# Loading x after the last memory units, and working the first two weight units as single k-tiles, in a two-layer decoder trunk on one Trainium2 core

## The reference

```python
def reference(x, mem, ...):
    for i in range(DEPTH):                       # DEPTH = 2
        h = _rms_norm(x, pre_norm[i])
        proj = h @ w_in[i]                       # 2048 x 7168
        ...                                      # short conv (layer 0) or differential attention (layer 1)
        mem_n = _rms_norm(mem, mem_norm[i])
        kv = mem_n @ w_kv_mem[i]                 # keys: columns 0-511, values: columns 512-1023
        ...                                      # cross-attention of 4 heads
        branch = jnp.concatenate([tok_out, cross_out], axis=-1) * jax.nn.silu(gate)
        x = x + _rms_norm(branch @ w_out[i], post_norm[i])
    return x
```

## Time and profile before

| what | value |
|---|---|
| time, median of 3 runs | 963.57 us (959.42 to 963.98) |
| time of the profiled execution | 964.46 us |
| its span, first to last instruction | 962.7 us |
| PE busy | 947.7 us, 98% of the span |
| PE weight loads busy | 813.1 us |
| DVE busy | 630.4 us |
| ACT busy | 475.4 us |
| moved by DMA | 182.31 MB, 189 GB/s in the mean |
| mean granted TensorE clock | 0.997 |

### The profile page before, as it was taken

How to read it: one execution, slowest core, us unless ns; L and a number is a source line. 1 busy time by engine, 2 the same in 40 slices (tenths; PEclk the granted TensorE clock), 3 DMA queues, 4 the chain that set the end, 5 groups by cost and what they waited for, 6 DMA issues and landing times.

```text
span 962.7 us, 14077 instructions
## 1 busy us (share of the span) xinstructions
PE 947.7 (98%) x5148; PEld 813.1 (84%) x5148; DVE 630.4 (65%) x867; ACT 475.4 (49%) x725; POOL 1.2 (0%) x9
## 2 busy tenths in 40 slices
PE   8899999999999999999999999999999999999996
PEld 7788888888888888888888888888888888888885
DVE  5677666656665656645596447457778878886555
ACT  6756634344434343344465445445465465554441
POOL 0000000000000000000000000000000000000000
PEclk9999999999999999999999999999999999999998
DMA  9657555666666656655666655565655765646562
GB/s 330 203 171 260 174 176 178 191 191 192 189 191 181 189 179 191 205 192 194 199 203 201 183 169 179 171 197 167 205 167 162 219 184 164 200 148 203 192 196 89
DMA packets 148762, 182.31 MB, mean 189 GB/s; under 512 B 8112, under 2 KB 116976, under 8 KB 147952
## 3 DMA queue, kind: packets, MB, share of 16 engines
q1 hardware_dynamic: 147776, 177.25, 59.2%
q10 hardware_dynamic: 944, 4.49, 1.2%
HBM read 176.48 MB, written 2.10 MB: 185 GB/s over the span
## 4 chain that ended last, share of the span: by engine, by line
PE 95%; DMA 2%; DVE 1%; ACT 0%; SPq 0%; issue 0%; DVEq 0%; ACTq 0%
PE psum L368 40%; PE psum L369 20%; PE psum L428 10%; PE psum L430 10%; PE psum L429 10%; DMA stage_area<-in_mem_dram 1%; PE psum L604 1%; PE psum L447 1%; PE psum L472 1%; PE psum L455 1%; DMA raw_ring<-in_w_kv_mem_dram 1%; DVE lo_ring L914 1%; PE psum L576 0%; PE psum L464 0%; ACT hi_ring L653 0%; PE psum L586 0%
## 5 line engine op out<-in xcount | busy, mean ns | idle before, releaser
L368 PE MATMUL psum<-hT_split,hi_ring 128*128 128x512 f32 x1600 | 564.4, 398 | 0.0
L914 DVE TENSOR_TENSOR lo_ring<-raw_ring,hi_ring 128x1024 fp32r<-128x1024 f32 x319 | 386.1, 1223 | 256.8 <-ACT hi_ring L653 255.0
L653 ACT ACTIVATE hi_ring<-raw_ring 128x1024 fp32r<-128x1024 f32 x319 | 336.4, 1062 | 398.1 <-PE psum L369 262.0
L369 PE MATMUL psum<-hT_split,lo_ring 128*128 128x256 f32 x1600 | 447.2, 279 | 0.0
L368 PEld LDWEIGHTS psum<-hT_split,hi_ring 128*128 128x128 f32 x1600 | 300.3, 188 | 72.8 <-issue 2.0
L369 PEld LDWEIGHTS psum<-hT_split,lo_ring 128*128 128x128 f32 x1600 | 301.7, 189 | 0.1
L428 PE MATMUL psum<-hi_ring,branchT_split 128*128 128x512 f32 x256 | 99.9, 390 | 0.0
L430 PE MATMUL psum<-hi_ring,branchT_split 128*128 128x512 f32 x256 | 99.6, 389 | 0.0
L429 PE MATMUL psum<-lo_ring,branchT_split 128*128 128x512 f32 x256 | 99.6, 389 | 0.0
L430 PEld LDWEIGHTS psum<-hi_ring,branchT_split 128*128 128x128 f32 x256 | 48.1, 188 | 10.1
L429 PEld LDWEIGHTS psum<-lo_ring,branchT_split 128*128 128x128 f32 x256 | 48.1, 188 | 10.0
(11 more groups left out here) (186 smaller groups left out, 671.8 us busy)
## 6 DMA issues: line engine op xcount, KB each, us to landing
raw_ring<-in_w_in_dram SPq DMA_DIRECT2D x224, 512.0 KB, 4.5
raw_ring<-in_w_out_dram SPq DMA_DIRECT2D x64, 512.0 KB, 4.9
raw_ring<-in_w_kv_mem_dram SPq DMA_DIRECT2D x31, 512.0 KB, 4.6
layer_area<-layer_area SPq DMA_DIRECT2D x48, 64.0 KB, 3.2
stage_area<-in_mem_dram SPq DMA_DIRECT2D x8, 256.0 KB, 7.1
x_residual<-in_x_dram SPq DMA_DIRECT2D x2, 1024.0 KB, 9.7
x_residual<-in_x_dram ACTq DMA_DIRECT2D x1, 2048.0 KB, 10.1
layer_area<-in_post_norm_dram ACTq DMA_DIRECT2D x2, 1024.0 KB, 5.4
```

Of the source, the lines that this page charges most:

```text
L368: mm(o, hi[:, k, P * c:P * (c + 1)], X[:, kt, :], start=kt == 0, stop=False)
L369: last = mm(o[:, SEQ:], lo[:, k, P * c:P * (c + 1)], X[:, kt, 0:SEQ], start=False, stop=kt == KT - 1)
L653: run(whi[:, slot, :], raw[:, slot, :], ACT.Copy).then_inc(hi_ready, 1)
L914: V_.tensor_tensor(wlo[:, slot, :], raw[:, slot, :], whi[:, slot, :].bitcast(f32), SUB)\
```

## The change

Three things are altered, all in `first_keys` and in what ACT, DVE and PE do beside it.

1. `load_x(0)` moves behind unit 6, `load_x(1)` behind unit 7.
2. Unit 1 is treated as unit 0 was: two DMAs of 256 KB, two split halves on ACT and on DVE, two k-tiles on PE with the transposes for unit 2 between them (before: ahead of the unit). The low parts of its two `memT_split` tiles have separate signals.
3. At the very start ACT splits the first half of unit 0 ahead of its norm wait and of `turned(0)`, and DVE takes the low part of that half ahead of the low part of the first tile. The second half of unit 0 is then split after `turned(0)`; on DVE it comes after both tiles.

```diff
-            load_mem(0)
-            sp.dma_start(raw[:, 0, 0:CROSS_WIDTH], w[:, 0, :]).then_inc(unit_begun, 16)
-            sp.dma_start(raw[:, 0, CROSS_WIDTH:], w[:, 1, :]).then_inc(raw_loaded[0], 16)
-            for n in range(1, STEPS):
+            for n in range(2):
+                load_mem(n)
+                sp.dma_start(raw[:, n, 0:CROSS_WIDTH], w[:, 2 * n, :]).then_inc(unit_begun[n], 16)
+                sp.dma_start(raw[:, n, CROSS_WIDTH:], w[:, 2 * n + 1, :]).then_inc(raw_loaded[n], 16)
+            for n in range(2, STEPS):
                 load_mem(n)
                 unit(n, n % SLOTS, raw[:, n % SLOTS, :].rearrange("p (k c) -> p k c", k=K_KT),
                      w[:, K_KT * n:K_KT * (n + 1), :])
-                if n in (5, 6):
-                    load_x(n - 5)
+                if n in (6, 7):
+                    load_x(n - 6)
...
-            pe.wait_ge(tile_turned, 1)
-            pe.wait_ge(lo_begun, 1)
-            k_tile(0, 0, range(4))
-            mem_turn(1)
-            pe.wait_ge(tr_lo, N_MEM0 + 1)
-            pe.wait_ge(lo_ready, 1)
-            k_tile(0, 1, range(4)).then_inc(unit_done, 1)
-            for n in range(1, STEPS - 1):
+            for n in range(2):
+                pe.wait_ge(tile_turned, n + 1)
+                pe.wait_ge(lo_begun, n + 1)
+                k_tile(n, 0, range(4))
+                mem_turn(n + 1)
+                pe.wait_ge(tr_lo, N_MEM0 + n + 1)
+                pe.wait_ge(lo_ready, n + 1)
+                k_tile(n, 1, range(4)).then_inc(unit_done, 1)
+            for n in range(2, STEPS - 1):
...
+        def first_high(n, half):
+            act.wait_ge(raw_loaded[n] if half else unit_begun[n], 16)
+            part = slice(CROSS_WIDTH * half, CROSS_WIDTH * (half + 1))
+            run(whi[:, n, part], raw[:, n, part], ACT.Copy).then_inc(hi_ready if half else hi_begun, 1)
+
+        first_high(0, 0)
         act.wait_ge(norm_ready, 1)
         turned(N_MEM0, XB, 2 * KT)
-        act.wait_ge(unit_begun, 16)
-        run(whi[:, 0, 0:CROSS_WIDTH], raw[:, 0, 0:CROSS_WIDTH], ACT.Copy).then_inc(hi_begun, 1)
-        act.wait_ge(raw_loaded[0], 16)
-        run(whi[:, 0, CROSS_WIDTH:], raw[:, 0, CROSS_WIDTH:], ACT.Copy).then_inc(hi_ready, 1)
+        first_high(0, 1)
         keep(0)
-        for n in range(1, STEPS):
+        first_high(1, 0)
+        turned(N_MEM0 + 1, XB, 2 * KT)
+        first_high(1, 1)
+        for n in range(2, STEPS):
...
-        dve.wait_ge(tr_hi, 1)
-        first_tile(0).then_inc(tile_turned, 1)
-        first_low(0)
-        first_tile(1).then_inc(tr_lo, 1)
-        first_low(1)
-        for n in range(1, STEPS):
+        first_low(0, 0)
+        first_tile(0, 0)
+        first_tile(0, 1)
+        first_low(0, 1)
+        first_low(1, 0)
+        first_tile(1, 0)
+        first_low(1, 1)
+        first_tile(1, 1)
+        keep(1)
+        for n in range(2, STEPS):
```

More of the change, by code:

```diff
@@ L188, in build @@
     mem_rows_loaded, pre_rows_loaded = sem("mem_norm_loaded"), sem("pre_norm_loaded")
-    unit_begun, hi_begun, lo_begun = sem("first_unit_half"), sem("first_hi_half"), sem("first_lo_half")
-    keys_half, tile_turned = sem("first_keys_half_done"), sem("first_tile_turned")
+    unit_begun = [sem(f"unit{n}_first_half") for n in range(2)]
+    hi_begun, lo_begun = sem("first_hi_halves"), sem("first_lo_halves")
+    keys_half, tile_turned = sem("first_keys_half_done"), sem("first_tiles_turned")
     gpost_loaded, out_stored = sem("gpost_loaded"), sem("out_stored")
@@ L999, in op, with first_tile, first_low @@
             st.need()
[L1001 to L1008, removed]
+        def first_tile(n, k):
+            dve.wait_ge(tr_hi, n + 1)
+            kt = 2 * n + k
+            V_.scalar_tensor_tensor(XB[:, kt, 256:512], ps[:, 4 + n, 256 * k:256 * (k + 1)],
+                                    gT[:, 2 * KT + kt:2 * KT + kt + 1], XB[:, kt, 0:256].bitcast(f32), MULT, SUB)\
+              .then_inc(tr_lo if k else tile_turned, 1)
+        def first_low(n, half):
+            dve.wait_ge(hi_ready if half else hi_begun, n + 1)
             part = slice(CROSS_WIDTH * half, CROSS_WIDTH * (half + 1))
-            V_.tensor_tensor(wlo[:, 0, part], raw[:, 0, part], whi[:, 0, part].bitcast(f32), SUB)\
+            V_.tensor_tensor(wlo[:, n, part], raw[:, n, part], whi[:, n, part].bitcast(f32), SUB)\
               .then_inc(lo_ready if half else lo_begun, 1)
```

## The result

The changed kernel takes 956.09 us (median of 6 runs, 955.9 to 956.39) where the kernel before, run again beside it, takes 964.1 (959.42 to 965.21, 6 runs): a ratio of 0.9919, with an interval of 0.9905 to 0.9933. The forecast was 961.6 and no measurable change; the medians lie 8.0 us apart. The times of the kernel before fall into two groups, 958.0 to 960.4 and 963.1 to 965.8 (one of its 121 executions lies between them), within every series of runs, and five of the six here are of the upper group. I call them the lower and the upper group.

What follows compares the result with a forecast made beforehand. PE was taken as the bound behind the first 37.64 us; there 3.2 us for the stall minus 1.2 for the head gave 2.0 us, moving the median from 963.57 to 961.6 us, range 957.8 to 964.2.

Steps and rivals of the forecast that it cites:

- The step that failed: PE, busy behind the first 37.64 us, is the bound; only that start can change, its saving passing unaltered to the end.
- the runs scatter: Rival: one of three runs took 959.42, four microseconds under the others; a median falling there gives 957.4 us; chance 0.15.
- The start: First 37.64 us: 3.2 us gained for the stall minus 1.2 for the head, 2.0 us in all.
- the last matmuls of the start move as a whole: From ACT's third sum of squares (26.67) to the first memory values matmul (37.64), one chain shifts unchanged, to 35.6.
- x behind the units: Unit 7's features, with one megabyte of x ahead instead of two, land at 23.9; ACT's 3.19 us stall goes to nothing.
- The new start: Reordered head: PE's first matmul 0.6 us later (8.47 for 7.85), ACT 1.21 us behind from unit 2's kept copy on.
- A second transfer for unit 1: The extra SP transfer costs nothing seen; a fixed 2.0 us in line, kept as rival, would leave a gain of 0.8 us.
- Unit 8: Landing left at 30.3, needed by about 32.0; rival: it becomes late, gain gone at 34.0, 965.6 us at 36; chance 0.06.
- the clock: Rival: PE's longer pause before its first k-tile lowers its clock, ending 4.7 us later at 968.3 us; chance 0.04.

Runs made afterwards that it cites:

- e6: Changed kernel with 17 instead of 16 transposes ahead of the mixer's loop of layer 0; ten executions at 961.1 to 962.2 us.
- e13: Changed kernel with 17 transposes ahead of the loop and one fewer idle transpose at the start; ten executions at 961.0 to 964.1 us.
- e4: Kernel before with 17 instead of 16 transposes ahead of the loop of layer 0; ten executions at 963.4 to 965.7 us.
- e11: Changed kernel with 17 transposes ahead of the loop and one small product behind them; ten executions at 961.0 to 962.8 us.
- e8: Kernel before with one small product (128x256) between the 16 transposes and the loop; ten executions at 958.2 to 960.3 us, ratio 0.9972.
- e9: Changed kernel with one small product between the 16 transposes and the loop; median 957.19 us of six, ratio to the kernel before 0.9937.
- e10: Changed kernel with a small product ahead of the loop and of layer 1's first keys' and first query groups; six executions at 956.3 to 958.7 us.
- e5: Changed kernel run again unaltered, beside the kernel before on the same chip; seven executions at 955.8 to 957.2 us, one at 961.4.
- e2: Changed kernel with x's transfers back behind units 5 and 6; nine executions at 958.4 to 961.4 us, one at 963.9.
- e7: Kernel before with 18 instead of 16 transposes ahead of the loop; six executions at 958.5 to 959.8 us, four at 963.8 to 965.2.
- e16: Changed kernel with PE's old order at unit 1, transposes for unit 2 first; seven executions at 956.1 to 958.0 us, three at 961.2 to 962.8.
- e3: Changed kernel with the old order of ACT and DVE at the very start; nine executions at 956.5 to 957.2 us, one at 961.8.
- e1: Kernel before with only x's two transfers moved behind units 6 and 7; four executions at 956.1 to 957.8 us, six at 961.1 to 962.4.

## Why the prediction was wrong

**The step that failed** is the first: "So only the first 37.64 us can change, and whatever they save or lose passes unaltered to the end: PE is the bound behind them." PE is the bound behind them, but being busy is not a fixed pace. The loop has two, and the profiled execution of before ran at the long one. 5.1 us of the 8.0 come from that. In the sum this term stood nowhere. The rival "the runs scatter" touched it and gave 957.4 with a chance of 0.15; it took the 959.42 for noise, where it was the other pace. The trace of before could have said so: the group ahead of the transposes, from 101.0 us on, runs its pairs at 346.7 ns, the loop behind them at 353.3. Three pairs of that group, to be held against the first four rows of the pattern above (1.04 us here, 1.06 there):

```profile
102.42 0.39 PE L368 MATMUL psum<-hT_split,hi_ring 128*128 128x512 f32 x1
...
103.46 0.39 PE L368 MATMUL psum<-hT_split,hi_ring 128*128 128x512 f32 x1
```

**What the runs showed in its place.** The pace of the loop is taken on at the restart behind the 16 transposes and kept for all 768 pairs (e6, e13). It is drawn in each execution, and its odds belong to the code. The short pace came in 54 of 121 for the kernel before, 13 of 14 for the changed one, none of 40 with 17 transposes (e4, e6, e11, e13), 22 of 22 with 16 transposes and a product (e8, e9, e10). So the comparison of medians had luck in it, too: one kernel was measured mostly in its upper group and the other in its lower one. With the medians of its two groups and its own odds the kernel before has 0.45 x 959.2 + 0.55 x 963.9 = 961.8 in the mean, and the changed kernel's fourteen executions have 956.6. The change is worth 5.2 us in the mean: 2.9 from the start (959.2 to 956.3, lower group against lower group) and 2.3 from the draw.

**The start** was sized nearly right, at 2.0 us. Within one series, that with e5, the lower groups are 958.6 and 956.3, 2.3 us apart, and the upper groups of before and of e6 963.8 and 961.6, again 2.3; in that of the result it is 964.2 - 956.1 less the 5.1 of the pace, 3.0. The step that the last matmuls of the start move as a whole is borne out best: in all eighteen traces the memory values begin 10.96 to 11.00 us behind the start of ACT's third sum of squares. That sum begins at 25.6 to 27.5 in the seven traces with x in its old place (26.5 in the mean) and at 23.2 to 25.5 in the eleven with x behind the units (24.3 in the mean, forecast 24.7), so the 3.5 us between the two profiled executions hold, by an estimate from these means, about 1.2 us of scatter. By steps:

- *x behind the units*, stall of 3.2 us to nothing: right for the changed kernel. After shows no idle time at the third sum of squares, e2 has 2.68 us of it again. But both ends scatter. With x in its old place the stall was 3.77 us in e8 and 0.86 in e7. The features landed at 14.67 + 7.5 = 22.2 in after, forecast 23.9; with x behind the units seven of the eleven traces still wait for them, 0.23 us (e16) to 1.42 (e10).
- *The new start*, 0.6 us for PE's first matmul and 1.2 us for ACT: right in its chain. From ACT's first split to its kept copy of unit 2 I had 16.08 - 6.36 = 9.7 us, measured 14.71 - 5.30 = 9.4; from the split to the memory values 29.2, measured 28.9. In absolute times all marks were missed by 1.2 to 1.5 us (7.23 for 8.4 to 8.5, 12.29 for 13.57, 18.36 for 19.7, 34.17 for 35.6), most of it since the first half unit landed at 5.3 in that execution and not at 6.36. e3 puts the cost of the new start itself at nothing that can be measured.
- *A second transfer for unit 1*: no fixed cost of 2 us in line is seen, which is what the row on the halves had said. e3 has that transfer and e1 has not, and the features let the third sum of squares begin at 24.60 and 25.14. The section that the prediction names from the Trainium skill (DMA: Bandwidth & Descriptors, "Anatomy of one DMA") gives its 2.0 us for transfers on the GpSimd path, and all of these are issued by SP.
- *Unit 8*: landed at 20.26 + 9.0 = 29.3, was split at 29.54 without a wait. The rival is out. So is the clock: 1.00 throughout.

**Open.** Why one transpose more fixes the long pace, why a product behind an even number fixes the short one and behind an odd number doesn't, and what in the treatment of unit 1, 100 us ahead, moves the odds. 17 is the only odd number that was run. Around the restart the rows of ACT and DVE of the two traces agree to 0.01 us after a shift of 3.46 us, and PE's own starts, those of the transposes included, stay 3.453 to 3.455 us apart up to the second pair of the loop; then the two patterns part. So what tips the choice isn't seen in these rows. The choice isn't peculiar to the loop: in the trace of before, unit 6 of the keys has the long pace (six pairs in 2.12 us from 31.33 on) and unit 7 the short one (2.08 us from 34.95 on), the first behind four transposes and 2.05 us of idle time, the second behind unit 6 and 0.53.

## What to carry to other kernels

Where an engine is busy for all of a stretch, measure its pace as well: divide the distance of two marks by the matmuls between them, and compare like loops within one trace. When the runs of one kernel lie in two groups, find the stretch that separates them before any change is forecast or judged, and compare groups with groups. A load that no one waits for can be late all the same, if an engine that works in order asks for it ahead of work on the critical path: look at whose queue it stands in front of.

## What the runs showed of the hardware

- The same 512 and 256 column matmuls, each with its weight load, run at 346.7 or 353.3 ns a pair at the same granted clock of 1.00, for up to 768 pairs on end, until PE does something else. Both are repeating patterns: 350, 361 and 349 ns, or 350 and 343, or 347 each (e8 to e10). The transposes ahead of them take 109 ns each in both cases.
- The loop's pace hangs on the number of transposes ahead of it: 17 gave the long pace in 40 of 40 executions, 16 or 18 gave both.
- The first 256 KB of weights, issued at 1.26 or 1.27 us in every kernel, landed 3.5 us later in one execution (e10) and 5.3 in another (e8). 256 KB of features, queued behind a megabyte of x, scattered by more: they had landed by 22.2 us in after, and in e10 ACT had to wait for them until 25.49. An early first landing alone decides nothing: e10 had the earliest, and its memory values begin at 36.49, the latest of the eleven traces with x behind the units.
